# A latent layer's second norm in two halves of tokens, with three tiles on either side of it by halves

## The reference, cut to what matters

```python
out_lat = mixer_merge(z_lat, attn_lat, ...)      # ends with  m @ w_out   (1024 x 1024)
x = x + g1 * out_lat
h2 = modulate(rmsnorm_2(x, norm2_g[l]), sh2, sc2)
x = x + g2 * conv_ffn(h2, ffn_up[l], ffn_conv_w[l], ffn_conv_b[l], ffn_down[l])

def rmsnorm_2(x, g):
    return x * lax.rsqrt(jnp.mean(x * x, axis=-1, keepdims=True) + EPS) * g
def modulate(h, shift, scale):
    return h * (1.0 + scale) + shift
def conv_ffn(h, w_up, cw, cb, w_down):           # w_up is 1024 x 5632
    u = dwconv3(h @ w_up, cw) + cb
    g, val = jnp.split(u, 2, axis=-1)
    return (jax.nn.silu(g) * val) @ w_down
```

## Time and profile before

| | |
|---|---|
| median of three runs | 3660.72 us |
| the profiled execution | 3661.29 us |
| its span, first to last instruction | 3659.5 us |
| mean granted TensorE clock | 0.972 |
| TensorE (PE) busy | 3504.9 us, 96% |
| weight loads (PEld) busy | 2919.5 us, 80% |
| VectorE (DVE) busy | 1488.5 us, 41% |
| ScalarE (ACT) busy | 1025.6 us, 28% |
| GpSimd (POOL) busy | 2025.0 us, 55% |

### The profile page before, as it was taken

One profiled execution on the slowest core, in us unless ns is written; L12 is line 12 of the kernel. 1 busy time (PEld: TensorE's weight loads), 2 busy tenths in 40 slices (PEclk: granted clock), 3 DMA queues, 4 the chain that ended last, 5 costly groups with the idle time before them and its releaser, 6 DMA issues. The chain is left out here.

```text
span 3659.5 us, 49562 instructions
## 1 busy us (share of the span) xinstructions
PE 3504.9 (96%) x19450; PEld 2919.5 (80%) x19450; DVE 1488.5 (41%) x3012; ACT 1025.6 (28%) x2757; POOL 2025.0 (55%) x1216
## 2 busy tenths in 40 slices
PE   7998989998999999899999999999999999999999
PEld 6876677877779988899777787888898777878887
DVE  7833541234873221452455214331333555224320
ACT  2245433133202110341344212220232444112210
POOL 4565353653559988745432465665554332656655
PEclk9999999989999999899999999999999999999999
DMA  7633132222764433332121222322222111223222
GB/s 283 209 125 106 61 95 96 90 87 79 238 216 146 150 129 114 141 110 93 53 64 47 75 92 81 96 94 94 102 92 79 61 58 47 92 81 98 92 88 97
DMA packets 109881, 388.88 MB, mean 106 GB/s; under 512 B 12057, under 2 KB 16537, under 8 KB 108242
## 3 DMA queue, kind: packets, MB, share of 16 engines
q1 hardware_dynamic: 89280, 315.10, 26.1%
q10 hardware_dynamic: 20370, 70.61, 5.4%
HBM read 379.34 MB, written 6.32 MB: 105 GB/s over the span
## 5 line engine op out<-in xcount | busy, mean ns | idle before, releaser
L2601 POOL CAST whi<-raw 128x1024 fp32r<-128x1024 f32 (+1 forms) x606 | 620.4, 1024 | 1573.7 <-DMA raw<-in_w 1573.3
L2603 POOL TENSOR_TENSOR wlo<-raw,whi 128x1024 fp32r<-128x1024 f32 (+1 forms) x606 | 1419.0, 2342 | 48.5
L363 PE MATMUL ps<-hhi,whi 128*128 128x512 f32 x1704 | 682.2, 400 | 18.5 <-DVE q L1600 8.5
L364 PE MATMUL ps<-hlo,whi 128*128 128x512 f32 x1704 | 676.2, 397 | 0.0
L365 PE MATMUL ps<-hhi,wlo 128*128 128x512 f32 x1704 | 676.0, 397 | 0.0
L363 PEld LDWEIGHTS ps<-hhi,whi 128*128 128x128 f32 x1704 | 321.9, 189 | 98.0 <-DVE q L1600 9.4
L365 PEld LDWEIGHTS ps<-hhi,wlo 128*128 128x128 f32 x1704 | 321.8, 189 | 77.8
L364 PEld LDWEIGHTS ps<-hlo,whi 128*128 128x128 f32 x1704 | 322.1, 189 | 74.4
L516 PE MATMUL ps<-whi,hhi 128*128 128x256 f32 (+1 forms) x960 | 275.5, 287 | 0.0
L518 PE MATMUL ps<-whi,hlo 128*128 128x256 f32 (+1 forms) x960 | 269.6, 281 | 0.0
L517 PE MATMUL ps<-wlo,hhi 128*128 128x256 f32 (+1 forms) x960 | 269.1, 280 | 0.0
(11 more groups left out here) (419 smaller groups left out, 7040.1 us busy)
## 6 DMA issues: line engine op xcount, KB each, us to landing
raw<-in_w SPq DMA_DIRECT2D x574, 512.0 KB, 3.6
ada<-in_ada ACTq DMA_DIRECT2D x96, 512.0 KB, 4.9
raw<-in_w SPq DMA_DIRECT2D x16, 384.0 KB, 3.5
att_toe<-toe_dram ACTq DMA_DIRECT2D x12, 256.0 KB, 3.3
raw<-in_w SPq DMA_DIRECT2D x16, 192.0 KB, 2.3
x<-in_x SPq DMA_DIRECT2D x4, 512.0 KB, 9.0
cond<-in_cc ACTq DMA_DIRECT2D x2, 1024.0 KB, 7.2
kc_dram<-kc ACTq DMA_DIRECT2D x2, 1024.0 KB, 5.0
```

The source lines that it names most:

```text
L363: nc.tensor.matmul(o, whi[:, buf, c], hi[:, k, 0:n], start=(k == 0), stop=False)
L364: nc.tensor.matmul(o, whi[:, buf, c], lo[:, k, 0:n], start=False, stop=False)
L2601: nc.gpsimd.tensor_copy(whi[:, buf, 0:c], raw[:, buf, 0:c]).then_inc(slab_hi, 1)
L2603: nc.gpsimd.tensor_tensor(wlo[:, buf, 0:c], raw[:, buf, 0:c], whi[:, buf, 0:c].bitcast(F32), ALU.subtract).then_inc(slab_split, 1)
```

## The change: what it does

The projection `L["o"]` keeps its first five tiles (`KT - ENDS`). Tiles 5, 6 and 7 go to a new part, `HalfTiles`: each is worked as two tiles of 256 tokens, in the order 5, 6, 7 for the first half of the tokens and then 5, 6, 7 for the second, with a residual on each. Their three slabs stay until the second half is done.

The norm becomes two norms of 256 tokens, `L["norm2", 0]` and `L["norm2", 1]`, with their statistics in banks 2 and 5 and shared buffers in banks 3 and 4; the second's first apply waits for the first's last low part (`after`). The running sum of squares now lies in the statistics bank, also in the first norm of layer 1, which uses the same class with `acc`.

The up product gets `lead=3`, and its first three tiles are worked by a new part, `Opening`. For the first half of the tokens it goes through tiles 0 and 1 together, one k at a time behind the norm's low parts, and then through all k of tile 2; for the second half it goes through the three tiles together, one k at a time. A tile is told done after its second half.

`mixer_end` writes the order out by hand, in place of `then_norm`. The rotation is `[0, 1, 6, 7]` from the half tiles on, and the wait for freed tiles ahead of layer 1's first norm covers four tiles of the down product instead of three.

```diff
-                self.lead = 2 if ready is not None and kt == BLOCKS else 1
+                self.lead, self.opened = (lead if lead else 2 if ready is not None and kt == BLOCKS else 1), False
...
+        class Opening(Part):
...
+            def tensor(self, pe, k):
+                g = self.gemm
+                if k == 0 and self.half == 0:
+                    for tile in g.tile[0:g.lead]:
+                        bank_ready(pe, tile)
+                if self.half == 0 and k == KT:
+                    for j in range(KT):
+                        self.block(pe, 2, j)
+                    return
+                pe.wait_ge(*self.norm.ready(k))
+                for t in range(2 if self.half == 0 else 3):
+                    self.block(pe, t, k)
+
+            def block(self, pe, t, k):
+                g, a = self.gemm, slice(TC * self.half, TC * self.half + TC)
+                s, o, c = g.slab[t][0], tile_out(g.tile[t], TC, TC * self.half), slice(k * P, (k + 1) * P)
+                if self.half == 0 and k == 0:
+                    pe.wait_ge(slab_split, s + 1)
+                nc.tensor.matmul(o, whi[:, s % RING, c], g.hi[:, k, a], start=(k == 0), stop=False)
+                nc.tensor.matmul(o, whi[:, s % RING, c], g.lo[:, k, a], start=False, stop=False)
+                mm = nc.tensor.matmul(o, wlo[:, s % RING, c], g.hi[:, k, a], start=False, stop=(k == KT - 1))
+                if self.half == 1 and k == KT - 1:
+                    mm.then_inc(tile_done, 1)
+
+        class HalfTiles(Part):
...
+            def tensor(self, pe, i):
+                if i < 2 * self.n_out:
+                    a = slice(TC * (i // self.n_out), TC * (i // self.n_out) + TC)
+                    feature_tile(pe, self.tile[i], [self.slab[i]], 0, KT, self.hi[:, :, a], self.lo[:, :, a], TC)
+
+            def vector(self, dve, i):
+                i -= 1
+                if i < 0:
+                    return
+                m, half, t = self.first + i % self.n_out, i // self.n_out, self.tile[i]
+                o = self.s.x[:, m, TC * half:TC * half + TC]
+                dve.wait_ge(tile_done, t + 1)
+                nc.vector.scalar_tensor_tensor(o, tile_out(t, TC), mod[:, self.gate + m, self.s.c:self.s.c + 1], o,
+                                               ALU.mult, ALU.add).then_inc(tile_free[tile_bank[t]], 1)
...
-                    square = self.sq[i % 2] if i or self.acc is None else self.bufs[0]
+                    square = self.sq[i % 2] if i or self.acc is None else self.stats[0]
...
-                    to = self.acc if i == K - 1 else self.bufs[0]
-                    nc.vector.tensor_tensor(to, self.bufs[0], self.sq[(i - 1) % 2], ALU.add).then_inc(self.ac, 1)
+                    to = self.acc if i == K - 1 else self.stats[0]
+                    nc.vector.tensor_tensor(to, self.stats[0], self.sq[(i - 1) % 2], ALU.add).then_inc(self.ac, 1)
...
                 if k == 0:
+                    for c in self.after:
+                        dve.wait_ge(*c())
...
-                all_free(layers[0]["down"], 3)
+                all_free(layers[0]["down"], 4)
...
-            L["o"] = Gemm(f"o{l}", KT, KT, m_hi, m_lo, T, Residual(lat, 48 * l + 16), ready=L["b"].ready)
...
+            L["o"] = Gemm(f"o{l}", KT - ENDS, KT, m_hi, m_lo, T, Residual(lat, 48 * l + 16), ready=L["b"].ready)
+            L["o_end"] = HalfTiles(f"o{l}", KT - ENDS, ENDS, m_hi, m_lo, lat, 48 * l + 16)
...
-            L["up"] = Gemm(f"f_up{l}", 2 * FF2, KT, hhi, hlo, T, gated, ready=L["norm2"].ready)
+            L["up"] = Gemm(f"f_up{l}", 2 * FF2, KT, hhi, hlo, T, gated, lead=3)
...
+        def mixer_end(o, end, first, second, up):
...
+            opens = Opening(up, 0, first), Opening(up, 1, second)
+            place(o, 0)
+            for i in range(1, KT - ENDS):
+                place(o, i)
+                go(first, i - 1)
+                go(second, i - 1)
+            rotate([0, 1, 6, 7])
+            go(end, 0)
+            go(o, KT - ENDS)
+            go(first, 4)
+            go(second, 4)
+            go(end, 1)
+            go(first, 5)
+            go(end, 2)
+            go(first, 6)
+            go(end, 3)
+            go(first, 7, 8)
+            go(end, 4)
+            go(second, 5)
+            go(first, 9)
+            go(end, 5)
+            go(second, 6)
+            go(first, 10)
+            go(end, 6)
+            place(Ends(second, 7), 0)
+            go(first, 11)
+            go(opens[0], 0, 1)
+            place(Products(second, 7), 0)
+            go(first, 12)
+            go(second, 8)
+            go(opens[0], 2, 3, 4)
+            place(Products(second, 9), 0)
+            go(first, 13, 14, 15, 16, 17)
+            go(opens[0], 5, 6, 7, 8)
+            place(Ends(second, 9), 0)
+            go(second, *range(10, second.steps))
+            go(opens[1], *range(KT))
...
-            then_norm(L["o"], L["norm2"])
+            mixer_end(L["o"], L["o_end"], L["norm2", 0], L["norm2", 1], L["up"])
```

More of the change, by code:

```diff
@@ L37 @@
 ADA_RING = 8
+ENDS = 3
 COLS = {}
@@ L386, in program, with __init__ @@
         class Gemm(Part):
-            def __init__(self, name, n_out, kt, hi, lo, n, epi, ready=None, first=0, clear=()):
+            def __init__(self, name, n_out, kt, hi, lo, n, epi, ready=None, first=0, clear=(), lead=0):
                 self.clear = clear
@@ L402, in place @@
                 if i < self.lead:
-                    if i == 0:
+                    if i == 0 and not self.opened:
                         for j in range(self.lead):
@@ L443, in vector, with __init__, place @@
                 self.epi.vector(dve, i)
+        class Opening(Part):
+            def __init__(self, gemm, half, norm):
+                self.gemm, self.half, self.norm = gemm, half, norm
+                self.steps = KT + 1 if half == 0 else KT
+            def place(self, k):
+                if k == 0 and self.half == 0:
+                    self.gemm.opened = True
+                    for j in range(self.gemm.lead):
+                        self.gemm.open(j)
+            def tensor(self, pe, k):
+                g = self.gemm
+                if k == 0 and self.half == 0:
+                    for tile in g.tile[0:g.lead]:
[17 more added lines that the diff above has]
+                    mm.then_inc(tile_done, 1)
@@ new lines, in program, with __init__, place, ready @@
+        class HalfTiles(Part):
+            def __init__(self, name, first, n_out, hi, lo, s, gate):
+                self.row0, self.first, self.n_out, self.hi, self.lo, self.s, self.gate = rows[name], first, n_out, hi, lo, s, gate
+                self.steps = 2 * n_out + 1
+                self.tile, self.slab = [], []
+            def place(self, i):
+                if i >= 2 * self.n_out:
+                    return
+                self.slab.append(new_slab(self.row0 + self.first + i, BLOCKS) if i < self.n_out else self.slab[i - self.n_out])
+                self.tile.append(new_tile([self.slab[i]]))
+            def ready(self, m, half):
+                return freed(self.tile[m - self.first + half * self.n_out])
+            def tensor(self, pe, i):
[5 more added lines that the diff above has]
+                if i < 0:
+                    return
+                m, half, t = self.first + i % self.n_out, i // self.n_out, self.tile[i]
[3 more added lines that the diff above has]
+                                               ALU.mult, ALU.add).then_inc(tile_free[tile_bank[t]], 1)
@@ L1015, in __init__ @@
             def __init__(self, name, src, mean, hi, lo, gain, shift, stats, bufs, sq, ready, group=None, clear=(), gained=(),
-                         acc=None):
-                self.n, self.gained, self.acc = stats[0].shape[-1], gained, acc
+                         acc=None, after=()):
+                self.n, self.gained, self.acc, self.after = stats[0].shape[-1], gained, acc, after
                 self.factor = norm_factor[name]
@@ L2450, in then_norm, with go @@
                 place(norm, i)
+        def mixer_end(o, end, first, second, up):
+            def go(part, *some):
+                for i in some:
+                    place(part, i)
+            opens = Opening(up, 0, first), Opening(up, 1, second)
[35 more added lines that the diff above has]
+            go(opens[1], *range(KT))
         ada0, ada1 = Ada(0, ada_ring, junk), Ada(1, ada_ring[0:4], junk, ADA_TILES // ADA_RING)
```

12 lines of the change are left out of this document (9 added, 3 removed).

## The result

Five runs of the changed kernel have a median of 3637.28 us (3635.68 to 3647.40), five of the kernel before, two of them new, 3659.27 (3652.15 to 3665.34). The ratio is 0.9944, interval 0.9930 to 0.9959: 20.5 us less, 15 to 26 by the interval. The profiled execution took 3637.46, with a span of 3635.6.

What follows compares the result with a forecast made beforehand. TensorE is busy 96% of the span, so only its stops and lower-clock stretches can give time. 46.32 + 43.55 - 2 x 37.8 = 14.3, less 1.2 for hand-offs, 13.1; from 3661.29, 3648.2: forecast 3648 us, range 3643 to 3656.

Steps and rivals of the forecast that it cites:

- How the numbers follow: Closing step on the whole kernel's time: chances of forecast and rivals, faster 0.77, and the range 3643 to 3656 us.
- the forecast without waits and hand-offs: Range's lower end: 3648 less 4.8 of TensorE waits and 1.2 of hand-offs in the changed regions, 3642 us.
- The mechanism: From `o` tile 5 to up tile 2, half tiles give TensorE work during the norm; 2.4 us of waits stay per layer.
- the layer's sum: Region from `o` tile 5 to up tile 2: 35.3 us of work plus 2.4 of waits, 37.8 per layer.
- The 0.6 per layer for hand-offs: Between low part and product in the opening: 0.2 us at each of three waits, added per layer.
- 13.1: Forecast saving in us over both layers' changed regions: 46.32 + 43.55 - 2 x 37.8 = 14.3, less 1.2 for hand-offs.
- layer 0's 46.32: Time before the change, in us, from `o` tile 5 to the end of up tile 2 in layer 0; layer 1 had 43.55.
- Clock (B): Rival: the clock falls in the up product's opening, 3 us per layer, 3651 with one layer, 3654 with both; chance 0.18.
- VectorE (C): Rival: VectorE bounds the opening, each operation 0.1 us late, 2 us per layer, 3652; chance 0.11.
- POOL (D): Rival: POOL's slab splits slow VectorE's norm operations in the opening, low parts 1.84 us instead of 0.48, about 3691; chance 0.05.
- nothing (E): Rival: waits between the hand-written steps as long as the old stop, so no gain, 3660 us; chance 0.06.
- The rule on small operations: For VectorE's norm operations: small tiles pay a fixed part each; 0.39 us per operation, 0.78 per tile, against 0.93 taken.

Runs made afterwards that it cites:

- the opening of two tiles: Changed kernel with two up tiles instead of three opened by halves, up tile 2 an ordinary full tile; ratio 0.9981 to the kernel before.
- layer 1 alone: The change in layer 1 only, layer 0 as in the kernel before; ratio 0.9979 to that kernel.
- layer 0 alone: The change in layer 0 only, layer 1 as in the kernel before; ratio 0.9994 to that kernel.
- the reordered kernel: Changed kernel with tile 1's low part ahead of the last residual and the second half's reciprocal one step later; ratios 0.9956, then 0.9925 to the kernel before.

## Why the prediction was wrong

**The step that failed is the range, in "How the numbers follow", which puts the stages beside the change at nothing.** Under "What would show it" stands "and all else as before", without a reason, and of the range the prediction says: "The lower end is the forecast without waits and hand-offs, 3648 - 4.8 - 1.2 = 3642, which I cut to 3643". Every term in it is of the changed stretches. None is for the 3050 us beside them, though a forecast of a time needs both. In the first profile these were 11.1 us shorter than before (3043.4 against 3054.4), almost as much as the changed stretches gave. They differ by 14.6 us between three profiles of one kernel (3043.4, 3051.7, 3058.0), and in the order of the mean granted clock (0.977, 0.976, 0.974). The three times shown spread over 6 us; 104 runs of the kernel before, over all chips, spread over 20 with a mean of 3659.3. The base was then one median of three, and the time to be met a median of five. The twelve runs of the same changed kernel in its third measurement have a median of 3646.07, inside the range.

**The mechanism was right, and so was the layer's sum.** From the end of half tile 7a in layer 0 (2196.66, 0.20 ahead of its residual), worked out and measured:

| | worked out | measured |
|---|---|---|
| spread | 6.33 | 6.44 |
| first apply | 7.08 | 7.08 |
| products of k=0 | 9.52 | 9.62 |
| products of k=1 (the longest wait) | 11.4 | 11.48 |
| reciprocal, second half | 13.48 | 13.56 |
| opening done | 29.6 | 29.66 |

The region from `o` tile 5 to up tile 2 is 8.16 + 29.66 = 37.8 us, the 37.8 of the forecast. The 0.6 per layer for hand-offs was not needed in layer 0. Two terms were off and cancel: statistics and spreads took 2.3 us where 2.7 stood, and half tiles 6b and 7b took 5.73 where 5.44 stood.

**That 13.1 met 12.8 has luck in it.** The sum took layer 0's 46.32 from one profile, in which its stretch had the longer of its two values. Without it both layers start from 43.5, and the sum is 2 x (43.55 - 37.8) - 1.2 = 10.3. Between the two repeated profiles the stretches give 10.9, and over eight unhalved and eight halved ones (means 301.8 and 296.0) 11.7 for two layers.

**Clock (B), one layer.** The prediction took 1.00, and rival B had 3 us for a layer in which the clock falls. It fell in two of eight halved stretches, for 1.5 us in layer 0 (296.92 against 295.4) and 1.0 in layer 1 (296.88 against 295.9). The event is real, and B's price was two to three times too high: 0.79 over 7 us and 0.98 over 13 are 3.5 us at the lower level, not the whole first half. The Trainium skill's sentence on short idling between groups of matmuls ("TensorE: Matmul & The Clock Gate", section "A second HAM failure mode: psum-queue depth-cycling") describes another kernel (bf16, 512 columns); these two of eight fit it, and six of eight went without. Layer 1 without a fall is 0.5 us longer than layer 0 (295.9 and 295.4). That lies in the 114 products behind the second spread: in the second profile of the changed kernel 13.01 us in layer 0 and 13.51 in layer 1, evenly, with the clock at 1.00 and VectorE at the same pace in both. Why is open.

**VectorE (C), POOL (D), nothing (E).** The pace was 0.91 per tile in both halves (2210.30, 2211.20, 2212.11 in VectorE's timeline are applies of the first half, 2216.13, 2217.04 and 2217.95 of the second), where 0.93 was taken. No low part beside a POOL subtraction took longer than its 0.48. The stop did not come back elsewhere.

**The size of the gain.** All 23 runs of the changed kernel have a mean of 3644.5 (standard error 1.4), the 104 of the kernel before 3659.3 (0.5): 14.8, give or take 2.8 at 95%. The forecast's 13.1 and the 12.8 of the first traces lie within that; the 11.7 of all profiles lie just below. That the 20.5 us of the first five runs were more than the change gives is shown by the repetitions (15.2 and 11.2 less by the means). In other kernels times and stretches agree within the interval: 7.6 less, give or take 2.8, for the opening of two tiles, whose stretches give 8.0; 7.5, give or take 4.0, for layer 1 alone and 2.8, give or take 3.6, for layer 0 alone, where 5.8 is usual of a stretch. Whether the remaining 3 us are chance is open, and so is why the reordered kernel's last five runs were lower than its stretches explain.

**The rule on small operations** (the Trainium skill, "VectorE: DVE Perf Modes", section "The TRN2 errata — SBUF-src ops pay a fixed extra latency per instruction"): by it the pace would have been 0.78 per tile (an estimate from that page); the trace has 0.91, and the rows of before were the better guide to it. Where the difference lies can be read in VectorE's timeline, layer 0, apply and low part in turn:

```profile
2210.30 0.47 DVE L1211 SCALAR_TENSOR_TENSOR ps<-x,gg,ps 128x256 f32<-128x256 f32 x1
2210.68 0.48 DVE L1220 SCALAR_TENSOR_TENSOR hlo<-ps,mod,hhi 128x256 fp32r<-128x256 f32 x1
2211.20 0.49 DVE L1211 SCALAR_TENSOR_TENSOR ps<-x,gg,ps 128x256 f32<-128x256 f32 x1
2211.60 0.48 DVE L1220 SCALAR_TENSOR_TENSOR hlo<-ps,mod,hhi 128x256 fp32r<-128x256 f32 x1
```

From an apply to the low part behind it there are 0.38 to 0.40 us, which is the 0.39 of the estimate. From a low part to the next apply there are 0.52: the low part's own 0.48 and 0.04 more. That fits a wait in the kernel: an apply writes the PSUM buffer that the low part just ahead of it reads, as there are two buffers, and starts only when that one is done. So the estimate had the distance between operations that don't wait for each other, and left out the buffer. What a third buffer would bring was not run.

**A version that beats both:** the low part first with the later reciprocal, 1.3 us shorter than the changed kernel in layer 0 (294.15 against 295.4) and 1.8 in layer 1 (294.14 against 295.9) where that kernel's clock held, up to 2.8 where it fell. Ratios to the kernel before are 0.9956 (0.9940 to 0.9971) and 0.9925 (0.9912 to 0.9939).

## What to carry to other kernels

Where a reduction over all outputs of one product gates the next, split along the axis that the reduction doesn't touch, on both sides of it: splitting the producer alone brought nothing here, because the consumer must have work of the first half for as long as the second half's chain takes. (Splitting the consumer alone was not run.) Write the engines' queues out on paper to a tenth of a microsecond before; here the moments held to 0.1 us over 30. Take the time before from several profiles: one in which a stop costs more than usual makes the gain look larger. And when a forecast becomes a range, add the spread of the stages that the change doesn't touch, from repeated runs, since it can be larger than all of the change's own terms.

## What the runs showed of the hardware that was not expected

The stages outside the changed stretches differ by up to 14.6 us of 3050 between executions of the same program, and the differences come in steps where the granted clock differs (0.93 or 0.77 over the same 60 us). A stop of about 8 us, with few matmuls in it, had two prices, 301.1 and 303.9 for the stretch around it, by how long the clock stayed at 0.50 behind it; behind a stop of 1.0 us between narrow matmuls the clock fell in two cases of eight (of ten, with the opening of two tiles). A run of 114 products of 256 columns at full clock took 13.01 us in one layer and 13.51 in the other, in the same execution.
